# Branch A's step order changed, first gates copied raw, input rows formed earlier, GpSimd subtractions cut in pieces

## What is computed

```python
h = layer_norm(x, ln_in_g, ln_in_b)
proj = h @ w_in[l]
qa, ka, va, qb, kb, vb, ga, gb = jnp.split(proj, pts, axis=-1)
...
s = jnp.einsum('bqhmd,bkhmd->bhmqk', qb, k).astype(jnp.float32) * scale + bias[None, :, None]
s = jnp.where(mask, s, NEG_INF)
p = jax.nn.softmax(s, axis=-1)
attn = p[:, :, 0] - lam * p[:, :, 1]
return jnp.einsum('bhqk,bkhe->bqhe', attn, vf)
...
merged = jax.nn.sigmoid(ga) * (ya @ w_branch_a[l]) + jax.nn.sigmoid(gb) * (yb @ w_branch_b[l])
h = layer_norm(DEEPNORM_ALPHA * h + merged @ w_out[l], ln1_g[l], ln1_b[l])
u = jnp.square(jax.nn.relu(h @ w_ff1[l]))
h = layer_norm(DEEPNORM_ALPHA * h + u @ w_ff2[l], ln2_g[l], ln2_b[l])
```

## Time and profile before

| | us |
|---|---|
| median of 3 runs | 1916.62 |
| range of these | 1914.64 to 1916.71 |
| the profiled execution, whole | 1914.67 |
| its span, first to last instruction | 1912.9 |
| TensorE busy in it | 1828.0 (96%) |
| VectorE, ScalarE, GpSimd busy | 911.4, 611.3, 547.3 |
| granted clock, mean of the span | 0.991 |

### The profile page before, as it was taken

The page is one execution under the profiler, slowest core; times in us unless marked ns, Lnnn a source line. Parts: engine busy times, 40 slices in busy tenths (PEclk is TensorE's granted clock), DMA queues, the critical chain, the costliest instruction groups (busy, mean ns, idle before and its releaser), DMA issues.

```text
span 1912.9 us, 24605 instructions
## 1 busy us (share of the span) xinstructions
PE 1828.0 (96%) x9175; PEld 1499.9 (78%) x9175; DVE 911.4 (48%) x2053; ACT 611.3 (32%) x1337; POOL 547.3 (29%) x329
## 2 busy tenths in 40 slices
PE   6999999999999997999999989999999999999995
PEld 4777777777778886888888768788888888888884
DVE  6466766667665552113413466433333333343337
ACT  5455555555556663211221301311111111111104
POOL 4211111111124341222222371633333333333324
PEclk9999999999999998999999999999999999999998
DMA  7311111111111100134222420311111111111102
GB/s 247 117 34 45 35 43 34 34 45 39 36 37 42 32 23 22 54 112 132 89 77 88 149 104 23 110 49 52 44 44 44 44 44 44 57 63 45 43 0 88
DMA packets 143140, 117.89 MB, mean 62 GB/s; under 512 B 23300, under 2 KB 129996, under 8 KB 143052
## 3 DMA queue, kind: packets, MB, share of 16 engines
q1 hardware_dynamic: 133836, 112.52, 18.7%
q10 hardware_dynamic: 9216, 4.20, 0.8%
HBM read 99.88 MB, written 21.53 MB: 63 GB/s over the span
## 4 chain that ended last, share of the span: by engine, by line
PE 80%; DVE 9%; ACT 5%; issue 3%; POOL 2%; DMA 1%; POOLq 0%; DVEq 0%; SPq 0%; ACTq 0%
PE bank L499 24%; PE bank L501 24%; PE bank L500 24%; PE bank L535 3%; PE bank L523 2%; PE bank L583 2%; ACT mix L890 1%; ACT mix L928 1%; DVE mix L1276 1%; DVE mix L1327 1%; PE bank L584 1%; DMA mix<-in_ln_in_b_dram 1%; DVE o_buf L1254 1%; DVE res L1202 1%; DVE small L1171 1%
## 5 line engine op out<-in xcount | busy, mean ns | idle before, releaser
L499 PE MATMUL bank<-hT_hi,w_hi 128*128 128x512 f32 x1312 | 527.4, 402 | 15.5 <-POOL w_lo L1041 6.0
L501 PE MATMUL bank<-hT_hi,w_lo 128*128 128x512 f32 x1312 | 514.0, 392 | 0.0
L500 PE MATMUL bank<-hT_lo,w_hi 128*128 128x512 f32 x1312 | 514.0, 392 | 0.0
L1041 POOL TENSOR_TENSOR w_lo<-w_raw,w_hi 128x1024 fp32r<-128x1024 f32 x66 | 159.0, 2409 | 688.6 <-ACT w_hi L772 688.5
L499 PEld LDWEIGHTS bank<-hT_hi,w_hi 128*128 128x128 f32 x1312 | 247.9, 189 | 77.8 <-issue 9.5
L501 PEld LDWEIGHTS bank<-hT_hi,w_lo 128*128 128x128 f32 x1312 | 248.0, 189 | 53.5
L500 PEld LDWEIGHTS bank<-hT_lo,w_hi 128*128 128x128 f32 x1312 | 248.4, 189 | 47.5
L499 PE MATMUL bank<-y_hi 128*128 128x512 f32 (+1 forms) x604 | 228.1, 378 | 2.7 <-DVE small L1467 2.7
L500 PE MATMUL bank<-y_lo,y_hi 128*128 128x512 f32 (+1 forms) x604 | 225.2, 373 | 0.0
L501 PE MATMUL bank<-y_hi,y_lo 128*128 128x512 f32 (+1 forms) x604 | 225.2, 373 | 0.0
L1450 DVE TENSOR_TENSOR res<-res,bank 128x512 f32<-128x512 f32 x224 | 154.1, 688 | 141.1 <-PE bank L501 141.1
(11 more groups left out here) (144 smaller groups left out, 2689.3 us busy)
## 6 DMA issues: line engine op xcount, KB each, us to landing
w_raw<-in_w_in_dram SPq DMA_DIRECT2D x100, 256.0 KB, 3.3
w_raw<-in_w_ff_dram SPq DMA_DIRECT2D x64, 256.0 KB, 3.0
mix<-in_w_ff_dram SPq DMA_DIRECT2D x16, 1024.0 KB, 7.1
bias_rows<-bias_line SPq DMA_DIRECT2D x3, 1536.0 KB
res<-in_x_dram SPq DMA_DIRECT2D x8, 512.0 KB, 6.7
x_spill<-res SPq DMA_DIRECT2D x8, 512.0 KB, 5.6
o_spill<-o_buf ACTq DMA_DIRECT2D x64, 64.0 KB, 1.6
w_raw<-in_w_branch_b_dram SPq DMA_DIRECT2D x16, 256.0 KB, 3.9
```

Source lines behind the costliest of these rows:

```text
L499: pe.matmul(bank, lhs[0], rhs[0], start=start, stop=False)
L500: pe.matmul(bank, lhs[0], rhs[1], start=False, stop=False)
L501: return pe.matmul(bank, lhs[1], rhs[0], start=False, stop=stop)
L1041: pool.tensor_tensor(w[1][:, n % 2], w_raw[:, :, :], w[0][:, n % 2].bitcast(F32), ALU.subtract).then_inc(w_lo_done, 1)
```

## The change

1. **Branch A.** In each step the first dense half now stands directly behind `block_a(0)`, then `block_a(1)`, then the transposes of block i-1, and then the product of the block **before** that one (two blocks on). The second dense half, where there is one, comes last. The head's value transposes move from block 0 to block 1. So that two blocks' probabilities can be alive, `pT` gets a second pair of buffers, which lies on `res` (the wait for the spill of x moves ahead of the branch on ACT). DVE's `combine` of a long block moves into the next step, between the reads of the first and the second piece of scores; ACT's exponentials of long blocks stand behind the copies of the transposed batch.
2. **Gates.** gb 0 and gb 1 are copied raw from PSUM; ACT applies the sigmoid to them from `res` later, in front of gb 2. The copy of gb 0 starts a step sooner, with `yb_high(0)`, `yb_low(0)` one step sooner too. The split of weight tile gb 2 is put ahead of the last copies. The square root over `sq_sum` moves behind the gb gates.
3. **Rows sooner.** `ln_in_g`, `ln_in_b` are loaded in front of the ma products, into `o_buf` and `bias_b_buf`; POOL forms row tiles 0, 1, 2 directly behind its w_out tiles 2, 4, 6. The first LayerNorm's vectors now go to `mix`, and the first MLP load of w_ff2, which takes their place, waits until that LayerNorm is done.
4. **GpSimd in pieces.** `w_lo` up to the MLP in 4 pieces of 128 x 256 in place of one of 128 x 1024, `hT_lo` in 2 of 256 in place of one of 512, w_out's low parts and the rows in pieces of 512.

```diff
+        p_more = nc.alloc_sbuf_tensor_at("p_more", [P, 2, SEQ], F32R, offset=y_at + 4 * KT * SEQ * 4)
...
-        pT = [y[1][:, 4 + r, :].rearrange("p (t q) -> p t q", q=P) for r in range(2)]
+        pT = [[t.rearrange("p (t q) -> p t q", q=P) for t in (s[:, r, :] for r in range(2))] for s in (y[1][:, 4:6, :], p_more)]
...
+        ln_in = [o_buf[:, :], bias_b_buf[:, :]]
+        ln_mid = [mix[:, 0, :], mix[:, 1, :]]
...
+                if kind == "ma" and i == 0:
+                    sp.wait_ge(scores_read, SCORE[("b", B_STEPS // NT - 1, NT - 1, 1, 0)] + 1)
+                    constants(ln_in_loaded, (ln_in[0], row(ln_in_g)), (ln_in[1], row(ln_in_b)))
...
                         sp.wait_ge(*wo_split(n))
-                    constants(ln_in_loaded, (ln_in[0], row(ln_in_g)), (ln_in[1], row(ln_in_b)))
-                    for n in (KT - 2, KT - 1):
-                        sp.wait_ge(*wo_split(n))
-                    sp.dma_start(ln_late[0], row(ln1_g)).then_inc(late_loaded, 16)
-                    sp.dma_start(ln_late[1], row(ln1_b)).then_inc(late_loaded, 16)
+                    sp.dma_start(ln_mid[0], row(ln1_g)).then_inc(late_loaded, 16)
+                    sp.dma_start(ln_mid[1], row(ln1_b)).then_inc(late_loaded, 16)
...
-                            sp.wait_ge(h_rows, NT)
+                            sp.wait_ge(ln_done, 2 * NT)
                         sp.dma_start(w2_raw, ff2[:, bass.ds(row_tile, 2), :]).then_inc(w2_loaded, 16)

             load_step(0)
-            sp.wait_ge(ln_done, 2 * NT)
+            sp.wait_ge(h_rows, NT)
...
                     block_a(0)
-                    prev = (h, i - 1) if i else (h - 1, NT - 1)
-                    if prev[0] >= 0:
-                        pe.wait_ge(probs_ready, prev[0] * NT + prev[1] + 1)
-                        for b in range(1 + prev[1] // 4):
-                            transposes(("pa",) + prev + (b,))
-                    if i >= 4:
-                        block_a(1)
-                    for _ in range(HALVES[i]):
+                    step = h * NT + i
+                    for piece in range(HALVES[i]):
                         group(*ORDER[6 * (h + 1) + at // 2], range(at % 2 * 4, at % 2 * 4 + 4))
                         at += 1
-                    if prev[0] >= 0:
-                        attend_a(*prev)
-                    if i == 0:
-                        pe.wait_ge(freed_act, freed(True, LAST[TILE[("va", h)]]))
-                        for b in range(2):
-                            transposes(("va", h, b))
+                        if piece == 0:
+                            if i >= 4:
+                                block_a(1)
+                            if step >= 1:
+                                pe.wait_ge(probs_ready, step)
+                                for b in range(1 + (step - 1) % NT // 4):
+                                    transposes(("pa", (step - 1) // NT, (step - 1) % NT, b))
+                            if step >= 2:
+                                attend_a((step - 2) // NT, (step - 2) % NT)
+                            if i == 1:
+                                pe.wait_ge(freed_act, freed(True, LAST[TILE[("va", h)]]))
+                                for b in range(2):
+                                    transposes(("va", h, b))
...
+            act.wait_ge(spilled, 16 * NT)
             for h in range(A_HEADS):
                 at = 0
                 for i in range(NT):
...
+                    step = h * NT + i
+                    if i < 4:
+                        exp_a(h, i)
+                    for piece in range(HALVES[i]):
                         if at % 2:
                             group_hi(*ORDER[6 * (h + 1) + at // 2])
                         at += 1
-                    if prev[0] >= 0:
-                        out_rows(prev[0] * NT + prev[1], *prev)
-                    if i == 0:
-                        for b in range(2):
-                            batch_hi(("va", h, b))
+                        if piece == 0:
+                            if step >= 1:
+                                for b in range(1 + (step - 1) % NT // 4):
+                                    batch_hi(("pa", (step - 1) // NT, (step - 1) % NT, b))
+                            if i >= 4:
+                                exp_a(h, i)
+                            if step >= 2:
+                                out_rows(step - 2, (step - 2) // NT, (step - 2) % NT)
+                            if i == 1:
+                                for b in range(2):
+                                    batch_hi(("va", h, b))
...
-                if s == B_STEPS - 1:
+                if s >= B_STEPS - 2:
                     act.wait_ge(yb_lo, 1)
-                    group_hi(TILE[("gb", 0)], 0)
+                    gate_raw(TILE[("gb", 0)], s - (B_STEPS - 2))
                 if s >= 1:
...
-                if s == B_STEPS - 3:
+                if s == B_STEPS - 4:
                     yb_high(0, B_STEPS - 5)
-            group_hi(TILE[("gb", 0)], 1)
             yb_high(1, B_STEPS - 1)
+            split_weights(TILE[("gb", 2)])
             probs_hi(B_STEPS - 1)
             o_rows_b(B_STEPS - 2)
             act.wait_ge(yb_lo, 2)
-            group_hi(TILE[("gb", 1)], 0)
+            gate_raw(TILE[("gb", 1)], 0)
             o_rows_b(B_STEPS - 1)
-            group_hi(TILE[("gb", 1)], 1)
+            gate_raw(TILE[("gb", 1)], 1)
...
-            act.wait_ge(sq_done, A_HEADS * NT)
-            act.activation(sq_sum[:, :, :], sq_sum[:, :, :], ACT.Sqrt, bias=eps, scale=1.0 / P).then_inc(y_norm, 1)
...
+                        if c == 2:
+                            act.wait_ge(freed_act, freed(True, POS[(TILE[("gb", 1)], 1)]))
+                            for n in range(2):
+                                act.activation(res[:, n, :], res[:, n, :], ACT.Sigmoid).then_inc(gates_set, 1)
...
+                if kind == "b":
+                    act.wait_ge(sq_done, A_HEADS * NT)
+                    act.activation(sq_sum[:, :, :], sq_sum[:, :, :], ACT.Sqrt, bias=eps, scale=1.0 / P).then_inc(y_norm, 1)
...
-                    pool.tensor_tensor(w[1][:, n % 2], w_raw[:, :, :], w[0][:, n % 2].bitcast(F32), ALU.subtract).then_inc(w_lo_done, 1)
+                    for at in range(0, KT, 2):
+                        ins = pool.tensor_tensor(w[1][:, n % 2, at:at + 2], w_raw[:, at:at + 2, :], w[0][:, n % 2, at:at + 2].bitcast(F32), ALU.subtract)
+                    ins.then_inc(w_lo_done, 1)
...
+                for at in range(0, HALF, HALF // 2):
+                    half_cols = slice(cols.start + at, cols.start + at + HALF // 2)
+                    ins = pool.tensor_tensor(hT[1][:, kt, half_cols], h_full[:, n % 4, at:at + HALF // 2], hT[0][:, kt, half_cols].bitcast(F32), ALU.subtract)
+                ins.then_inc(h_lo, 1)
...
+            def rows_in(t):
+
+                pool.wait_ge(res_loaded[t], 16)
+                for at in range(0, DM, HALF):
+                    ins = pool.tensor_tensor(res[:, t, at:at + HALF], res[:, t, at:at + HALF], ln_in[0][:, at:at + HALF], ALU.mult)
...
+            pool.wait_ge(ln_in_loaded, 32)
             for n in WO_POOL:
                 pool.wait_ge(wo_hi, n + 1)
-                pool.tensor_tensor(y[1][:, n, :], mix[:, n % 4, :], y[0][:, n, :].bitcast(F32), ALU.subtract).then_inc(wo_lo[0], 1)
-            pool.wait_ge(ln_in_loaded, 32)
-            for t in range(NT):
+                for at in range(0, DM, HALF):
+                    ins = pool.tensor_tensor(y[1][:, n, at:at + HALF], mix[:, n % 4, at:at + HALF], y[0][:, n, at:at + HALF].bitcast(F32), ALU.subtract)
+                ins.then_inc(wo_lo[0], 1)
+                rows_in(WO_POOL.index(n))
+            for t in range(len(WO_POOL), NT):
+                rows_in(t)
...
+            def combine(n):
+
+                i, slot = n % NT, n % 2
+                dve.wait_ge(exp_done, n + 1)
+                if n >= 4:
+                    dve.wait_ge(sq_done, n - 3)
+                link(dve.reciprocal(inv[:, n % 4, :], sums[:, slot, :]))
+                link(dve.scalar_tensor_tensor(coef[:, slot:slot + 1], sums[:, slot, 0:1], neg_lam, inv[:, n % 4, 1:2], ALU.mult, ALU.mult))
+                p = [s_a[:, slot, m, 0:(i + 1) * P] for m in range(2)]
+                dve.scalar_tensor_tensor(p[0], p[1], coef[:, slot:slot + 1], p[0], ALU.mult, ALU.add).then_inc(probs_ready, 1)
+                dve.sem_inc(inv_ready, 1)
...
+                        if c == 0 and i > 4:
+                            combine(step - 1)
...
+                    if i == 0 and h:
+                        combine(step - 1)
+                    for piece in range(HALVES[i]):
                         if at % 2 and TILES[ORDER[6 * (h + 1) + at // 2][0]][0] not in FREED_BY_ACT:
                             qk_lo(*ORDER[6 * (h + 1) + at // 2])
                         at += 1
-                    if prev[0] >= 0:
-                        sum_halves(step - 1)
-                    if i == 0:
```

(19 more changed lines are left out.)

84 lines of the change are left out of this document (35 added, 49 removed).

## The result

The changed kernel takes **1892.53 us** (median of 4 runs, 1891.27 to 1893.98), against 1916.66 for the kernel before in the same comparison: a ratio of 0.9876, 95% interval 0.9859 to 0.9893. It is 24 us faster, where 37 were forecast; it lies half a microsecond above the range, 1866 to 1892. The profiled execution took 1891.27, its span 1889.5 at a granted clock of 0.992.

The account below looks back on a forecast made before the run. The prediction took PE as the bound, with time to gain only from its waits: branch A 18, gates 13, projection 7, less 1 for pieces, 37 us in all, giving 1879 us; the 8-in-10 range was 1866 to 1892.

Parts of the forecast that it names:

- starts of divided halves: Branch A: each separated dense half starts slowly, 0.1 us a start, four blocks in each of 8 heads, 3.2 us lost.
- (a): Branch A, block 1: the first transpose's wait for DVE's low part of the values, 8.4 us in all, goes.
- (b): Branch A: transposes of block i-1 waiting for DVE's combine, 4.9 us in all, are covered by a dense half.
- (c): Branch A: the second piece of scores waiting until a bank is read, 4.4 us in all, goes.
- margin of 0.4 us in blocks 5 to 7: Branch A: DVE's reads and combine end 2.9 us after the scores, PE arrives after 3.3 us or more.
- 17.7 us of waits for 28: Branch A: PE's printed waits of 17.7 us were taken to cost 1.6 times that, 28 us, all to go.
- w_lo at block 3: Branch A: the tile for blocks 3 and 4 comes later, 0.4 us a head, 3.2 us lost.
- the lock on the combine: Branch A: the moved combine meets POOL's w_lo pieces, 0.4 us a head, 3 us lost, ends 0 and 8.
- Rival 1: Branch A gives only 5 us if the 0.4 us margins fail and transposes wait as before: 1892 us; chance 0.14.
- rival 4: Branch A: lock or late exponentials stretch each of 32 long steps, so the change is slower, 1927 at 1.5 us; chance 0.02.
- Rival 5: Cutting does not loosen the DVE-POOL lock; projection loses 3.4, branch A some 3 us: 1886; chance 0.14 with rival 2.
- rival 2: Projection: POOL's rows stretch under the lock, tile 4 late, clock falls, no gain there: 1886; chance 0.14 with rival 5.

Follow-up runs that it names:

- e5_w_whole: The changed kernel with GpSimd's w_lo subtractions of all tiles in one instruction again, other cuts kept: 1914.32 us, ratio 0.9989 to the kernel before.
- e6_hi_first: The changed kernel with ACT's copy ahead of its exponentials in branch A's blocks 1 to 3, DVE's low part moved ahead too: 1886.13 us, ratio 0.9851.
- e8_sum: The changed kernel with ACT's copy ahead of the exponentials in blocks 1 to 3, the start's subtractions whole, rows after all w_out tiles: 1880.17 us, ratio 0.9820.
- e7_pairs: The changed kernel with both dense halves of a block ahead of the transposes in branch A's blocks 0 and 5 to 7: 1897.81 us, ratio 0.9908.
- e9_pieces_old: The kernel before with only GpSimd's w_lo subtractions cut in four pieces: 1915.88 us, ratio 1.0006.

## Why the prediction was wrong

Two steps of branch A failed. The list of what comes back had no term for a chain over ACT and DVE in the short blocks, which made new waits of 9 us; and what the old waits cost, with the starts of divided halves, was put at 24.8 us where the traces show 18.1.

**Branch A: 18 forecast, 3.0 measured.** The steps, one by one:

- (a), (b) and (c), the three waits that a dense half was to cover, went. The margin of 0.4 us in blocks 5 to 7 held with the pieces, though the combine over 896 keys took 1.54 us in the mean, not 1.15; with w_lo whole it did not hold (0.58 us a head, `e5_w_whole`).
- *The missing term*, 9 us. The prediction read DVE's order in the long blocks only, where the combine moved. In blocks 0 to 3 it moved nothing on DVE, but the change swaps `exp_a` and `batch_hi` on ACT there, and I gave that no sentence. It put ACT's copy and DVE's low part behind the exponentials, DVE stood idle for 1.97 us in block 3's step, and block 4's scores paid. `e6_hi_first` shows it, by undoing the swap and nothing else but the place of DVE's low part. Undoing it took the 9 us of waits away and gave 4.8 us at full clock, since 3 us came back as other waits.
- *The mis-sized terms*. I took 17.7 us of waits for 28, at 1.6 times what is printed, and the starts of divided halves for 3.2: 24.8 us together if every wait went. To test it I counted each of the 2664 matmuls of branch A from its start to the start of the next, less the idle time, at full clock. The kernel before has 20.2 us of idle time (the smallest gaps counted too) and 458.0 of work, the changed kernel 13.4 and 460.1, `e8_sum` 8.5 and 460.8. So with every wait gone the new order would have gained 20.2 us less 2.1 of added work: 18.1 us, not 24.8. Within the work, the dense matmuls rose from 271.9 to 282.3 us and the transposes fell from 45.9 to 36.2, by what stands next to them. How much of that belongs to a wait can't be told apart, so 1.6 stays a guess for the branch, made from one row.
- Starts of divided pairs alone: 3.2 forecast. 31 pairs are divided, for head 0's block 0 has nothing in between; joining them took 5.7 us from the dense matmuls in `e7_pairs` (282.3 to 276.6), 0.18 us a pair, and the products behind them got 2.9 us longer.
- w_lo at block 3: 3.2 forecast, 2.1 measured; the lock on the combine: 3 forecast, and no wait of PE for the combine is left in the branch.
- Not forecast: 1.6 us at the last block, and one stretch of half clock in the branch (449.7 to 453.1), 1.7 us.

The sum closes: 24.8 less 3.2 and 3 was the forecast of 18.6; 18.1 less 13.4 of waits and 1.7 of clock is the 3.0 measured. About 7 of the 15 us missed are waits beyond the forecast, the missing term above all, about 7 are the mis-sized terms, and 1.7 the clock. So even with the swap undone and the clock full (`e8_sum`) the branch gave 8.9 us, and not 18.

Of the signs that the prediction named, the one against it came true: PE's waits in branch A kept a sum of 13 us, above its 8.

**Rival 1 gave the right number for the wrong place.** It said 1892 if the margins in the long blocks failed. They held, and the number is luck; the short blocks, which it did not look at, gave the wait. Its one argument, a DVE queue that does more between scores and combine, is not what happened: DVE did less and waited more. And "DVE has 150 us idle in the branch", my case against rival 4, says nothing about a chain: DVE's share of busy time counts its waits for ACT as room.

**Rival 4 and the lock.** The mechanism of rival 4, steps stretched by a lock and late exponentials, is what `e5_w_whole` shows, 11.7 us of it in branch A, though more of it in the short blocks than in the long ones that rival 4 named. Without the pieces the changed kernel takes 1914 us. I had valued the lock at 0 to 8 us, by DVE's rows of the old order, in which it cost PE nothing (`e9_pieces_old`). Rival 5 is refuted: in pieces the small operation falls from 761 to 300 ns.

**Gates: 13 forecast, 15.3 measured.** Both waits and both stretches of half clock went. Of the step "0 for branch B" the sign was off: it saved 2.9 us, 2.5 of them by the pieces (`e5_w_whole`), and the gates got 1.7 by them, for DVE's small operations there, which POOL's scalings wait for, are no longer held by a whole w_lo.

**Projection: 7 forecast, 5.3 measured.** The first read came right behind PE (1095.17, 1.29 us) and DVE's shifts fell from 3.21 us to 2.12. But a row tile took 7.1 us on POOL, not 5; DVE's subtractions of 2.1 and 2.3 us ran beside it, and alone its four pieces take 5.0. So tile 4 came 3.5 us late, not tile 6 by 2.2, and the clock fell. That was rival 2's mechanism, at half its price.

**Start: -1 forecast, -3.1 measured**, of which the cuts can't be shown to be the cause.

## What to carry to other kernels

When a change swaps two operations on one engine, follow the *other* engine that waits for the later one through a whole step, and compare the length of that chain with the step of the engine that should be the bound; a share of busy time does not show it. An operation cut in pieces, so that a shared lock is let go sooner, may be worth nothing where the blocked engine has cover and everything where a new order takes that cover away, so try such a pair of edits together and apart. Where work is put into a queue ahead of something that TensorE needs, count it at the length that it has under contention.

## What the runs showed of the hardware

- A DVE operation on 128 x 2 numbers with one input tile took 1.62 us, and 0.17 elsewhere, beside a POOL operation of 2.38 us, and ended 0.03 us behind it.
- Four pieces of w_lo on POOL take 2.79 us where one takes 2.36, 0.14 us a cut, at the start of the kernel; in branch A a piece lasts 0.83 us in the mean in the changed kernel and 0.74 in `e9_pieces_old`.
- Executions of one kernel differed by 12 us: those of `e5_w_whole` went from 1904 us at a mean clock of 0.995 to 1916 at 0.989. The clock lost, 0.005 of 1902 and 0.011 of 1914 us, differs by 11.5 us, so it accounts for nearly all of it. The four of `e8_sum` stayed within 2.5 us.
- Equal code at the start took 67.4 to 70.9 us in four executions, and 67.7 to 71.0 in five of the changed kernel's start.
